# Moving 52 weight-sum transfers of a fused block from the first gate and up to the mixing and attention stage

## The reference, cut to what matters

```python
x = x + 0.5 * swiglu(rmsnorm(x, g_ffn1), w1_gate, w1_up, w1_down)   # first gate, up and down
h = rmsnorm(x, g_mix)
p = h @ w_in                                                         # "mixing"
out_a = dsa_sparse_attention(qa, ka, va, qi, ki, wi)                 # index scores, top 128 keys, heads of 64
out_b = mla_attention(cq, ckv, kr, ...)                              # latent attention, 8 heads
x = x + concatenate([out_a, out_b]) @ w_out
x = x + 0.5 * swiglu(rmsnorm(x, g_ffn2), w2_gate, w2_up, w2_down)   # second gate, up and down
return rmsnorm(x, g_final)
```

## Time and profile before

| | |
|---|---|
| median of 3 runs | 1974.95 us (1971.78 to 1975.82) |
| the profiled execution | 1976.35 us, span 1974.4 us |
| PE matmul busy | 1884.8 us, 95% of the span |
| DVE, ACT, POOL busy | 1106.6, 673.3, 378.3 us |
| q0 (GpSimd's DMAs) | 100.31 MB, 19.7% of 16 engines' span |
| q1 (SP's DMAs) | 384.24 MB, 54.3% |

### The profile page before, as it was taken

The page is one execution under the profiler, slowest core; times in us unless marked ns, Lnnn a source line. Parts: engine busy times, 40 slices in busy tenths (PEclk is TensorE's granted clock), DMA queues, the critical chain, the costliest instruction groups (busy, mean ns, idle before and its releaser), DMA issues. The chain is left out here.

```text
span 1974.4 us, 26524 instructions
## 1 busy us (share of the span) xinstructions
PE 1884.8 (95%) x9569; PEld 1346.0 (68%) x9570; DVE 1106.6 (56%) x1668; ACT 673.3 (34%) x1030; POOL 378.3 (19%) x452
## 2 busy tenths in 40 slices
PE   8999999998997799998999999999999899999998
PEld 7888888785332233333688877887665589999886
DVE  4998993444111111111643336765697638777897
ACT  4234435432000000000422214562336746444466
POOL 2023233201221122222023331002145500010100
PEclk9999999999999999999999999999999999999999
DMA  6489999997999999999477996676310025666565
GB/s 200 149 294 289 251 326 236 296 388 302 424 425 426 426 427 424 394 426 422 138 242 243 244 240 188 190 181 169 94 66 12 1 66 159 182 181 180 173 198 171
DMA packets 202680, 485.84 MB, mean 246 GB/s; under 512 B 34892, under 2 KB 113153, under 8 KB 177370
## 3 DMA queue, kind: packets, MB, share of 16 engines
q1 hardware_dynamic: 171802, 384.24, 54.3%
q0 software_dynamic: 30768, 100.31, 19.7%
q10 hardware_dynamic: 16, 0.00, 0.0%
HBM read 475.17 MB, written 111.67 MB: 297 GB/s over the span
## 5 line engine op out<-in xcount | busy, mean ns | idle before, releaser
L559 PE MATMUL psum<-h_hi,w_hi 128*128 128x512 f32 (+1 forms) x1240 | 452.3, 365 | 10.0 <-DVE w_lo L554 7.0
L561 PE MATMUL psum<-h_hi,w_lo 128*128 128x512 f32 (+1 forms) x1240 | 447.0, 360 | 0.0
L560 PE MATMUL psum<-h_lo,w_hi 128*128 128x512 f32 (+1 forms) x1240 | 446.9, 360 | 0.0
L554 DVE TENSOR_TENSOR w_lo<-w_raw,w_hi 128x1024 fp32r<-128x1024 f32 (+1 forms) x144 | 179.3, 1245 | 306.1 <-ACT w_hi L549 305.9
L549 ACT ACTIVATE w_hi<-w_raw 128x1024 fp32r<-128x1024 f32 (+1 forms) x144 | 151.6, 1053 | 513.4 <-PE psum L561 426.6
L559 PEld LDWEIGHTS psum<-h_hi,w_hi 128*128 128x128 f32 x1240 | 235.4, 190 | 51.5 <-DVE w_lo L554 9.8
L560 PEld LDWEIGHTS psum<-h_lo,w_hi 128*128 128x128 f32 x1240 | 235.5, 190 | 35.4 <-issue 1.4
L561 PEld LDWEIGHTS psum<-h_hi,w_lo 128*128 128x128 f32 x1240 | 235.2, 190 | 35.5
L1407 PE MATMUL psum<-arena,w_raw 128*64 128x512 f32 x800 | 181.7, 596 | 13.2 <-DMA arena<-in_w_expert_up_dram 12.4
L1542 ACT ACTIVATE w_raw<-psum 128x256 f32<-128x256 f32 x36 | 13.8, 384 | 461.6 <-PE psum L1407 461.6
L1069 DVE SCALAR_TENSOR_TENSOR arena<-arena,vec 128x512 f32<-128x512 f32 x240 | 162.6, 749 | 1.0 <-ACT arena L896 1.0
(11 more groups left out here) (396 smaller groups left out, 3213.4 us busy)
## 6 DMA issues: line engine op xcount, KB each, us to landing
arena<-in_w_expert_gate_dram SPq DMA_DIRECT2D x44, 1024.0 KB, 20.1
arena<-in_w_expert_up_dram SPq DMA_DIRECT2D x44, 1024.0 KB, 25.5
arena<-in_w_expert_down_dram SPq DMA_DIRECT2D x22, 2048.0 KB, 29.0
weight_terms<-in_w_down_dram POOLq DMA_DIRECT2D x60, 512.0 KB, 8.1
w_raw<-in_w_in_dram SPq DMA_DIRECT2D x44, 512.0 KB, 8.1
expert_down_third<-in_w_expert_down_dram SPq DMA_DIRECT2D x10, 2048.0 KB, 28.3
expert_input<-in_w_expert_gate_dram SPq DMA_DIRECT2D x20, 1024.0 KB, 22.6
expert_input<-in_w_expert_up_dram SPq DMA_DIRECT2D x20, 1024.0 KB, 26.5
```

What stands on the lines that cost most here:

```text
L554: eng.tensor_tensor(wlo[:, s, :, 0:n], raw[:, slot, :, 0:n], whi[:, s, :, 0:n].bitcast(F32), ALU.subtract).then_inc(w_lo, 1)
L559: eng.matmul(o, w_h, x_h, start=first, stop=False)
L560: eng.matmul(o, w_h, x_l, start=False, stop=False)
L561: return eng.matmul(o, w_l, x_h, start=False, stop=last)
```

## The change

`STEPS_PER_GROUP` and `GROUPS_WITH_STEPS` become 0, so the 45 steps 108 to 152 leave the first gate and up. All steps 108 to 159, 52 of them, are now issued in `pool_mix`: 7 at its head, 5 after the second rotary product, 7 after the sixth, 8 after the tenth, 4 after the sums of squares, one behind every second division of the 32 B units (16), and the last 5 behind the last division. The order of the steps among themselves and the wait of each are as they were.

```diff
-STEPS_IN_FIRST, STEPS_PER_GROUP, GROUPS_WITH_STEPS = 108, 5, 9
+STEPS_IN_FIRST, STEPS_PER_GROUP, GROUPS_WITH_STEPS = 108, 0, 0
+STEPS_IN_MIX = {0: 7, 2: 5, 6: 7, 10: 8, 13: 4}
+STEPS_BY_UNIT = 2
@@
         def pool_mix(pool):
             pool.wait_ge(tables_in, 48)
             pool.wait_ge(w_used, C_MIX)
-            for n in range(STEPS_IN_FIRST + STEPS_PER_GROUP * GROUPS_WITH_STEPS, ALL_STEPS):
-                term_step(pool, n)
+            steps = iter(range(STEPS_IN_FIRST + STEPS_PER_GROUP * GROUPS_WITH_STEPS, ALL_STEPS))
+
+            def some_steps(after):
+
+                for n in itertools.islice(steps, STEPS_IN_MIX.get(after, 0)):
+                    term_step(pool, n)
+
+            some_steps(0)
             for r in range(R_QA):
                 group_read(pool, G_MIX + rot_group[r])
                 if r >= 3:
                     pool.wait_ge(mx["rope"], r - 2)
                 pool.tensor_tensor(cos_at(r), ropes[r][0], cos_of[ropes[r][1]], ALU.mult).then_inc(mx["cos"], 1)
+                some_steps(r + 1)
@@
             pool.wait_ge(mx["lat_sum"], 3)
+            some_steps(R_QA + 3)
             pool.wait_ge(mx["acc"], 2 * N_IDX)
@@
                 pool.tensor_scalar(p_u, p_u, p_inv[:, u % NP:u % NP + 1], None, ALU.mult).then_inc(at_["p_pool"], 1)
+                if u % STEPS_BY_UNIT == 1 and u < NB:
+                    for n in itertools.islice(steps, 1):
+                        term_step(pool, n)
+            for n in steps:
+                term_step(pool, n)
```

More of the change, by code:

```diff
@@ L1 @@
+import itertools
 from contextlib import ExitStack
```

## The result

| | before | after | ratio |
|---|---|---|---|
| first comparison, 8 runs of each | 1974.49 us | 1979.59 us (1976.54 to 1986.59) | 1.0033 [1.0021, 1.0044] |
| changed kernel again, 21 runs of before, 11 of it | 1975.61 us | 1977.37 us (1975.76 to 1980.27) | 1.0014 [1.0005, 1.0023] |

The times are medians, with the range of the changed kernel's runs behind them; the ratio is one of means, with a 95% interval. The changed kernel is slower, by 1.8 and 5.1 us by the medians, and by 1 to 9 us by the two intervals. The forecast was no change (1974.6 us, from a sum of -0.4 us). The time lies in the range, but the sign of the sum was wrong.

The account below looks back on a forecast made before the run. PE was taken as the bound, with GpSimd close behind in attention. A gain of 8.6 us and a loss of 8.2 us sum to -0.4, so 1974.95 - 0.4 = 1974.6 us, range 1968.3 to 1981.5.

Parts of the forecast that it names:

- The gain in the first gate and up: First gate and up: with 45 steps gone, PE's 38 missing matmuls come back, a gain of 8.6 us (7.9 to 9).
- Rival 3: First gate and up: the stall isn't only the steps' and part stays, net +2 to +5 us; chance 0.07.
- 31 steps in mixing: Mixing: the steps fit behind GpSimd's idle times of 22.0, 30.9 and 32.0 us, cost nothing.
- The four before the key copies: End of mixing: the key copies move from 1447.5 to about 1455, with 8 us of slack left, cost nothing.
- The 16 steps between divisions: B units of attention: late landings on the DMA engines shift GpSimd and PE, 8.2 us lost (bounds 2 to 14).
- The issue alone: B units of attention: issues of 0.81 us, four per round, lengthen four rounds by 1.6 us each, 6.4 us.
- The last five steps: Behind the last division: they land by about 1603, a landing up to 15 us later would be hidden, cost nothing.
- Rival 1: Attention: DMA is faster alone and only issues count, loss 2 to 6.4 us, net -6.6 to -2.2; chance 0.23.
- Rival 2: Attention: accumulating steps hold GpSimd longer and PE's clock gives way, net +4 to +9 us; chance 0.2.

Follow-up runs that it names:

- e1: Changed kernel with 20 copying steps back in the first gate and up, 31 accumulating ones in mixing, one behind the last division, none between divisions: 1973.17 us, ratio 0.999.
- e6: Changed kernel with 18 useless matmuls on PE ahead of its wait for the division of unit 20: 1978.11 us, ratio 1.002.
- e10: Kernel before, with steps 128 to 152 copying instead of adding, all in their places, sums incomplete: 1967.65 us, ratio 0.996.
- e7: Kernel before, but with 25 steps in the first gate and up, 24 in mixing, none between divisions, 3 behind the last: 1967.26 us, ratio 0.9961.
- e8: Kernel before, but with 25 steps in the first gate and up, 18 in mixing, 8 behind divisions of A units, 1 at the end: 1967.36 us, ratio 0.9961.
- e9: Kernel before, but with 25 steps in the first gate and up, 18 in mixing, 8 between divisions of B units, 1 at the end: 1968.24 us, ratio 0.9960.
- e3: Changed kernel whose 16 steps between divisions move an eighth of the columns, sums incomplete: 1973.35 us, ratio 0.9991.
- e5: The changed kernel unchanged, run again for more runs and a second profile: 1977.37 us, ratio 1.0014.
- e4: Changed kernel whose 16 steps between divisions copy instead of adding, sums incomplete: 1970.49 us, ratio 0.9971.
- e2: Changed kernel with 20 copying steps back in the first gate and up, 16 steps in mixing, 16 still between divisions: 1978.88 us, ratio 1.0024.

## Why the prediction was wrong, point by point

- **The gain in the first gate and up.** Forecast 8.6 us, measured 8.60 in the changed kernel, and the same within 0.02 in every other kernel that has no accumulating steps there (e1 to e6, e10) or five at most (e7, e8, e9). Counting missing matmuls was the exact way; the count by gaps and clock gave 8.3. Rival 3 is out.
- **31 steps in mixing.** Forecast nothing, measured -0.1 to -0.3. The reason given, GpSimd's idle times, wasn't the one that decides: e1 has as many steps at each place, accumulating ones at the first two, and loses 5.1 us because the chunks of `w_in` come late, not because GpSimd does. I had named the place where that would show, and hadn't worked out its margin.
- **The four before the key copies.** As forecast. GpSimd stands 5.42 us ahead of the last of them, starts the copies at 1449.62 and has 8.24 us left before PE releases it (in the earlier trace rows it had 15.78):

```profile
1448.76 0.81 POOL L2261 DMA_DIRECT2D up_terms<-in_w_gate_dram  x1 [5.42 <-issue]
1449.62 5.00 POOL L3255 COPY arena<-arena 32x512 f32<-32x512 f32 x8
1462.86 4.95 POOL L3259 TENSOR_TENSOR arena<-arena,const 128x512 f32<-128x512 f32 x4 [8.24 <-PE psum L2794]
```

- **The 16 steps between divisions: the step that failed.** Forecast 8.2 us, measured 10.0 and 10.5. The working was "13 transfers x 3.53 = 45.9 us" plus 2.4 of lag until step 151 has landed, and that this landing sends step 154 out, 48.3 us after step 139. They stand 50.5 us apart (1495.29 and 1545.79 above), 9.6 more than the 40.9 of the earlier trace rows; with some 0.6 for the last one's own issue that is 10.2, PE's shift. The transfers weren't slower than I took them: in the stretch from 1494 to 1560 us GpSimd's queue moved 16 steps in 88.4% of 66 us, 3.65 us each, or 3.4 us each by 0.721 MB at 212 GB/s.

```profile
q0 software_dynamic: 2304, 11.54, 88.4%
```

  Step 151, issued at 1533.78, took 10.7 us to land:

```profile
DMA to landing us min/median/max: 10.7/10.7/10.7
```

  That is 1544.5, 49.2 us after step 139. So the lag in my sum was 49.2 - 45.9 = 3.3 us, 0.9 more than the 2.4 I took and still under the 3.9 that I had called its upper end. The other 1.3 us of the 50.5 are the real fault of the step: step 154 went out 1.3 us after the landing, with no idle time before it in its row, straight behind GpSimd's pair of divisions at 1542.72. The landing on which the whole working rested wasn't what held it. I had taken issues and landings as two alternative bounds for the whole stretch and used the larger. But the issues fill GpSimd in the first two rounds (10.48 of 10.72 us, 12.89 of 13.05), one gap of 2.84 us ahead of a step stands in the third, and in the fourth GpSimd is busy for 12.54 of 13.77 us and stands ahead of no step. The shift is larger than either bound (8.2 us by landings, 6.4 by issues) and smaller than both together.
- **The issue alone.** Forecast 6.4 us, measured 5.6 (e3), near by luck. An accumulating issue between divisions took 1.2 us at the median in the changed kernel and 1.75 in e3, not 0.81. And more of it than I allowed overlaps the division behind it (rows of 1517.67 and 1518.28 above: 0.87 us of issue, but 0.61 to the next start). The two errors went in opposite directions.
- **The last five steps.** As forecast. They are issued by 1592.7, SP's first load behind them starts at 1606.88, 3.03 us later than in the earlier trace rows, and the last division is later by the same 3.03 (1581.74 and the earlier trace rows's 1578.71). The rest of the kernel takes the same 382.73 us.

```profile
1583.41 2.60 POOL L2261 DMA_DIRECT2D up_terms<-up_terms  x3
1591.01 1.64 POOL L2261 DMA_DIRECT2D up_terms<-up_terms  x2 [4.99 <-DMA up_terms<-up_terms]
```

```profile
1606.88 0.37 SPq L1953 DMA_DIRECT2D w_raw<-in_w_gate_dram  x1
```

- **Rival 1**, issues alone, is refuted for the whole: with all bytes moved the loss is 10.0 us, and 5.6 when only the issues are left (e3). An accumulating step takes 3.4 to 3.65 us of the engines and lands 9 to 12 us after its issue. By the fit of the Trainium skill ("DMA: Bandwidth & Descriptors", section "Anatomy of one DMA — SWDGE (gpsimd) path"), 2.0 us plus the bytes over 436 GB/s, a step would be an estimated 1.65 us of engine time; the trace disagrees, and it decides.
- **Rival 2**, slower by a longer service and a fall of the clock, had the sign right and the price wrong. The gap of 3.2 us and the fall both came, but PE was waiting for GpSimd in that stretch, and in e6, without the fall, only 0.2 to 0.7 us come back. Nor was a step's service longer.

The sum with measured terms is -8.6 + 10.2 = +1.6 us where I had -0.4. That agrees with the second comparison. That the time came so near to the forecast owes much to two terms of 8 to 10 us that cancel. What stays open is the remaining 3 us of the first comparison: in its profiled execution 1.7 us lie in the head, where the kernel is the same, beside a stretch of 6.8 us at 1.2 GHz at 448 us that the kernel before hadn't. e5 had that stretch too, at 446 us, and no longer head. I ran nothing on it, and don't count it as an effect of the change.

## What to carry to other kernels

Work that is put into the gaps of a helping engine costs little as long as it fits in the slack of one round, of that engine and of each resource that it draws on, and far more beyond that: 8 steps cost 0.8 us, 16 cost 10. Work out the slack per round first (here 10.6 - 8.55 us of GpSimd and 10.6 us of DMA), and when two bounds are close, don't take the larger for the whole stretch. Follow the chain step by step, and ask at each whether the engine or the landing comes last; here the truth (10.0) lay above both bounds (8.2 and 6.4). Before moving transfers off a saturated stretch, ask what saturates it: here moving 20 of the 45 steps (e7) gave the full 8.6 us. Replacing the additions by copies without moving anything gave it too (e10), which names the cause but isn't a remedy, since the sums are then incomplete.

## What the runs showed of the hardware that I had not expected

- A transfer from DRAM to DRAM that accumulates takes the DMA engines 3.4 to 3.65 us per 0.721 MB (after); with copies in place of the additions the share of the engines falls from 1.06 to 0.77 (e10).
- Between divisions its issue on GpSimd takes 0.86 us at the median with 8 of them in the stretch (e9), 1.2 with 16 (after), and 1.75 with 16 of an eighth of the bytes (e3), while a copy's takes 0.57 (e4).
- A single accumulating step lands 6.4 us after its issue at the median, and 6.2 at the least, even with hardly anything beside it (e9).
- Gaps of PE of 3.2 and 3.3 us were followed by 1.2 GHz (after, e1), as the 3.11 of the earlier trace rows was; so was one of 1.85 us in e2, but not the 2.02 of the earlier trace rows. Where GpSimd bounded the stretch, keeping the clock up gave back 0.2 to 0.7 us (e6).
